# Hybrid decoder step on one core: cached keys scored by page groups of all sequences, with queries as weights and the compression on two row halves

## The reference, cut to what matters

```
k_cmp, v_cmp, k_sel, v_sel = cached pages (4096 rows) + new rows      # 2 key heads x 64
h  = silu(first half of a 32-row block @ w1[:1024] + second half @ w1[1024:] + pe @ w1)
kc, vc = h_k @ w2_k, h_v @ w2_v                      # 255 blocks of 32 rows, stride 16
p_cmp = softmax(q . kc + bias);   o_cmp = p_cmp @ vc
block importance from p_cmp -> top 16 blocks of 64 rows
o_sel = softmax over the chosen blocks of q . k_sel;  o_win = softmax over the last 512 rows of q . k_win
o = gate0*o_cmp + gate1*o_sel + gate2*o_win
```

## Time and profile before

| | us |
|---|---|
| median of 3 runs | 3118.72 (3117.09 to 3127.64) |
| the profiled execution | 3124.01 |
| its span, first to last instruction | 3122.1 |
| `sample_scores`, layer 1, first transpose to last copy | 278.7 to 580.0 |
| the same, layer 2 | 1815.3 to 2115.7 |
| PE busy over the span | 2809.9 (90%) |
| DVE, ACT, POOL busy | 1064.2 (34%), 680.6 (22%), 221.2 (7%) |
| DMA | 274 MB, mean 88 GB/s |

### The profile page before, as it was taken

The page is one execution under the profiler, slowest core; times in us unless marked ns, Lnnn a source line. Parts: engine busy times, 40 slices in busy tenths (PEclk is TensorE's granted clock), DMA queues, the critical chain, the costliest instruction groups (busy, mean ns, idle before and its releaser), DMA issues. The chain is left out here.

```text
span 3122.1 us, 40922 instructions
## 1 busy us (share of the span) xinstructions
PE 2809.9 (90%) x14512; PEld 2232.4 (72%) x14512; DVE 1064.2 (34%) x2653; ACT 680.6 (22%) x1592; POOL 221.2 (7%) x242
## 2 busy tenths in 40 slices
PE   6997999699598999999969889996986989999997
PEld 4875777567585788888758677774665858888886
DVE  2833555445444210000118245554445332100002
ACT  0113444223421110000111244442233103000002
POOL 0500000000040100000005000000001201000000
PEclk8997999889795999999979989997996969999998
DMA  6214556144001225023042065532420011340220
GB/s 192 70 41 156 168 168 188 41 125 122 3 3 27 82 68 162 27 54 81 0 134 81 23 203 189 175 124 67 121 81 2 21 57 58 95 122 25 70 54 29
DMA packets 334997, 274.00 MB, mean 88 GB/s; under 512 B 52866, under 2 KB 330563, under 8 KB 334459
## 3 DMA queue, kind: packets, MB, share of 16 engines
q1 hardware_dynamic: 308296, 251.58, 27.0%
q10 hardware_dynamic: 26546, 20.35, 2.2%
HBM read 262.01 MB, written 18.17 MB: 90 GB/s over the span
## 5 line engine op out<-in xcount | busy, mean ns | idle before, releaser
L2190 PE MATMUL psum<-xT,up_ring 128*128 128x272 f32 x2048 | 470.3, 392 | 0.0
L2190 PEld LDWEIGHTS psum<-xT,up_ring 128*128 128x128 f32 x2048 | 389.4, 190 | 80.0
L2209 PE MATMUL psum<-ff,HT 128*128 128x272 f32 x1536 | 353.6, 393 | 0.0
L2209 PEld LDWEIGHTS psum<-ff,HT 128*128 128x128 f32 x1536 | 292.1, 190 | 59.9
L366 PE MATMUL psum<-xT,w_ring 128*128 128x272 f32 x1408 | 327.0, 395 | 7.0 <-PEq L161 4.0
L366 PEld LDWEIGHTS psum<-xT,w_ring 128*128 128x128 f32 x1408 | 269.6, 192 | 64.2 <-issue 4.7
L1015 PE MATMUL psum<-chunks,W 128*128 128x512 f32 x512 | 242.2, 635 | 10.6 <-DVE chunks L1137 10.6
L1137 DVE COPY chunks<-psum 64x256 f32<-64x256 f32 x512 | 215.2, 420 | 28.9 <-PE psum L994 21.6
L994 PE MATMUL psum<-cst,cache 128*128 128x128 f32 x1536 | 193.5, 278 | 20.8 <-DMA cache<-in_cache_nsa_kv 20.6
L2053 DVE SCALAR_TENSOR_TENSOR xT<-xT,psum 128x544 f32<-128x544 f32 (+1 forms) x42 | 24.2, 585 | 529.7 <-PE psum L2209 441.6
L1015 PEld LDWEIGHTS psum<-chunks,W 128*128 128x128 f32 x512 | 102.5, 203 | 138.6 <-issue 138.6
(11 more groups left out here) (421 smaller groups left out, 3307.2 us busy)
## 6 DMA issues: line engine op xcount, KB each, us to landing
cache<-in_cache_nsa_kv SPq DMA_DIRECT2D x512, 192.0 KB, 3.3
up_ring<-in_w_up SPq DMA_DIRECT2D x32, 1024.0 KB, 5.3
vsel<-in_cache_nsa_kv SPq DMA_DIRECT2D x384, 64.0 KB, 1.9
HT<-in_w_down SPq DMA_DIRECT2D x12, 2048.0 KB, 9.0
w_ring<-in_w_in SPq DMA_DIRECT2D x20, 1024.0 KB, 5.1
vsel<-in_cache_nsa_kv ACTq DMA_DIRECT2D x128, 64.0 KB, 2.3
HT<-in_w_out SPq DMA_DIRECT2D x8, 1024.0 KB, 6.7
yT<-in_w_down SPq DMA_DIRECT2D x4, 2048.0 KB, 10.5
```

Source lines behind the costliest of these rows:

```text
L2190: last = pe.matmul(psum[:, 2 * (t % 4) + h, 0:HALF], up_ring[:, g % 3, k, (t % 2) * P:(t % 2) * P + P], xT[:, k, half_of(h)], start=(k == ...
L2209: last = pe.matmul(psum[:, 2 * (t % 4) + h, 0:HALF], down[t % 3][:, k, :], f[:, k, half_of(h)], start=(k == 0), stop=(k == FT - 1))
```

## The change

Work is regrouped from sequences to page groups. A unit is 4 pages of one sequence; 8 units (one per sequence) cover the same 4 page numbers of all sequences, four units make a quad, 16 quads make the layer, and two more quads hold the window keys. Everything is written out; there is no loop over sequences. In a quad TensorE makes for each unit 12 transposes into banks 0, 1, 2 (one set in place of two), and after each unit's transposes a quarter of the compression of the quad before; after the second unit it also scores the quad before.

- Scores: the queries of a sequence are the weights (32 columns: 16 of them, and zeros in place of the other sequence of the pair), the 512 turned keys are the moving data, and the four units of a quad write four strips of 32 rows of one PSUM bank. Two quads accumulate into the same bank, so it then holds the scores of all 128 query rows, and one copy by VectorE takes them.
- Compression: 64 rows per matmul. Head 0 uses rows 0 to 63 and head 1 rows 64 to 127 of the array, with weights stored twice, and the two heads write two banks. 128 moving columns: 32 blocks of each of the four units.
- `chunks` is filled by one copy of 128 rows in place of four of 64.
- Blocks at a group's edge need the last block of the group before: a small `carry` tile and two small GpSimd adds per quad.
- The prompt's compression and the position term become "quad -1" of the same stage and leave `natural_keys`. Stage "q" goes; GpSimd places the queries in `natural_keys`, and copies out the values that the attention needs later.
- The weights of the first layer are loaded twice (8 DMAs in place of 4).
- "top" gains the second layer of the values (16 matmuls) and loses two transposes; "soft" loses 36 transposes, and adds the block bias in one instruction of 4096 columns.

```diff
 def compression_loads(S, l, sp, s):
-    sp.dma_start(S.pe_n[:, :], layer(io.cmp_pe, l).rearrange("c (h j t) d -> (c h j) (t d)", h=2, j=8)).then_inc(s.cmp, 16)
+    for k in range(KVH):
+        sp.dma_start(S.pe_n[:, HD * k:HD * k + HD], layer(io.cmp_pe, l).rearrange("c p d -> (c p) d")).then_inc(s.cmp, 16)
...
+            for k in range(KVH):
+                sp.dma_start(S.W1[HD * k:HD * k + HD, c, :, HD * h:HD * h + HD], src).then_inc(s.cmp, 16)
...
 def natural_keys(S, l, ctx):
+            for k in range(KVH):
+                r = slice(64 * k, 64 * k + 64)
+                for g in range(GRP):
+                    q = H(T_Q + g)[r, SEQ:].rearrange("p (b t) -> p b t", b=NB)
+                    pool.tensor_copy(rows[r, :, k, g, :], q).then_inc(s.placed, 1)
+                    for o in range(2):
+                        pool.tensor_copy(pads[r, o, o, :, k, g, :], q[:, o::2, :]).then_inc(s.placed, 1)
...
+            pool.tensor_copy(S.kvn[:, :, 0:P], kvn[:, :, 3 * P:4 * P]).then_inc(s.values, 1)
...
 def sample_scores(S, l, ctx):
+    gp, slots = 4, 3
...
+            def turn(u):
+                pe.wait_ge(loaded[u % slots], arrived[u])
+                for bank, c in enumerate((2, 0, 1)):
...
+                    for j in range(gp):
+                        last = pe.transpose(psum[:, bank, j * P:j * P + P], cache[:, u % slots, j, c * P:c * P + P], C["ident"])
+                last.then_inc(s.turned, 1)
+
+            def score(q):
...
+                for i in range(4):
+                    u = 4 * q + i
+                    last = pe.matmul(psum[32 * i:32 * i + 32, 3, :], S.q_pad[:, seq(u), :], kts[u % 8], start=(q % 2 == 0), stop=(q % 2 == 1))
+                last.then_inc(s.scored, 1)
+
+            def compress(q, part):
+                c = part // 2
...
+                n = NP if q < 0 else P
+                for j in range(8 * (part % 2), 8 * (part % 2) + 8):
+                    for k in range(KVH):
+                        r = slice(HD * k, HD * k + HD)
+                        last = pe.matmul(hidden(q, k, c), W1[r, c, j, :], chunks[q % 2][r, c, j, 0:n],
+                                         start=(j == 0), stop=(j == 15))
...
+            for q in range(NQD + 2):
+                for i in range(4):
+                    turn(4 * q + i)
+                    if i == 1 and q:
+                        score(q - 1)
+                    if q <= NQD:
+                        compress(q - 1, i)
+            for i in range(4):
+                keys(i)
+            prompt_second()
+            score(NQD + 1)
+            cmp_score()
...
 def sample_softmax(S, l, ctx):
+            for i in range(4):
+                j = i // 2
+                for n in range(4):
+                    b = 4 * (i % 2) + n
+                    last = pe.matmul(psum[:, 4 + i, n * P:n * P + P], S.hid[:, 1, b, j * P:j * P + P], S.W2[:, 1, :], start=True, stop=True)
...
-            for q in range(NQ):
-                dve.wait_ge(s.turned, q + 1)
-                dve.tensor_tensor(p_sel[:, 512 * q:512 * q + 512].rearrange("p (j n) -> p j n", n=64),
-                                  psum[:, q % 4, :].rearrange("p (j n) -> p j n", n=64), bc(block_bias[:, 8 * q:8 * q + 8], 64),
-                                  ALU.add).then_inc(s.added, 1)
+            x = p_sel[:, 0:PAST].rearrange("p (j n) -> p j n", n=64)
+            dve.tensor_tensor(x, x, bc(block_bias[:, 0:NBLK], 64), ALU.add).then_inc(s.added, 1)
```

More of the change, by code:

```diff
@@ L803, in natural_keys @@
     H = lambda t: S.HT[:, t - 6, :]
[L804 to L813, removed]
+    kvn = sb("kv_rows", [P, QT, 6 * P], ctx=ctx)
@@ L835, in _ @@
                              C["ident"][0:M_W, 0:M_W]).then_inc(s.turned, 1)
[L836 to L849, removed]
         @block.scalar
@@ L856, in _ @@
                 act.wait_ge(s.turned, q + 1)
[L857 to L864, removed]
+                act.copy(dst, psum[0:n, 2 * (q % 4), :]).then_inc(s.copied_act, 1)
             act.wait_ge(s.copied_dve, QT + 1)
@@ L876, in _ @@
                 dve.wait_ge(s.turned, q + 1)
[L877 to L888, removed]
-                                      ALU.add).then_inc(s.added, 1)
-            dve.wait_ge(s.second, 2)
-            dve.tensor_copy(kc[:, :], psum[:, 6, 0:31]).then_inc(s.kept, 1)
-            dve.tensor_copy(vc[:, :], psum[0:31, 7, 0:P]).then_inc(s.kept, 1)
+                dve.tensor_copy(dst, psum[0:n, 2 * (q % 4) + 1, 0:256])
+                dve.tensor_copy(S.misc_n[0:n, q, :], psum[0:n, 2 * (q % 4) + 1, 256:256 + M_W]).then_inc(s.copied_dve, 1)
         @block.sync
@@ L912, in sample_scores @@
     H = lambda t: S.HT[:, t - 6, :]
-    S.q_rows = sb("q_rows", [P, P], ctx=ctx)
-    S.st_cmp = sb("st_cmp", [P, 2, P], ctx=ctx)
-    with stage(nc, "q", "zero", "placed") as (block, s):
+    gp, slots = 4, 3
+    NQD = 2 * (NPG // gp)
+    NU = 4 * (NQD + 2)
+    W1, W2, hid = S.W1, S.W2, S.hid
+    cache = sb("cache", [P, slots, gp, 3 * P], ctx=ctx)
+    second = sb("chunks", [P, 2, 16, P], ctx=ctx)
+    chunks = (S.st_sel[:, :, :].rearrange("p (c j) n -> p c j n", c=2), second)
+    kts = ([S.vc[:, j, 4 * i:4 * i + 4, :].rearrange("p b n -> p (b n)") for j in range(2) for i in range(2)]
+           + [S.yT[:, 4 + i, 0:4 * P] for i in range(4)])
@@ new lines, in sample_scores @@
+    kcs = [cache[:, i, :, :].rearrange("p j n -> p (j n)")[:, 0:512].rearrange("p (b n) -> p b n", b=2) for i in range(2)]
+    kcs += [second[:, i, 0:4, :].rearrange("p j n -> p (j n)").rearrange("p (b n) -> p b n", b=2) for i in range(2)]
+    hb = S.st_win[0:HD, :, :].rearrange("p (k c) n -> p k c n", k=KVH)
+    carry = sb("carry", [HD, 2, 2, KVH, 2, 4], ctx=ctx)
+    hc = sb("hc", [P, 2, 31], ctx=ctx)
+    NP = 34
+    names = ("turned", "k_copied", "v_copied", "sel_act", "sel_dve", "scored", "sc_copied", "tok", "pe_turned", "pe_copied",
+             "comp", "half", "added", "carried", "kept", "zero", "swish", "p_added", "pe_h", "p_swish", "p_second", "p_kept",
+             "kc", "kc_act", "kc_dve", "cmp_scored", "loaded0", "loaded1", "loaded2")
@@ new lines, in add @@
+            def add(q):
+                dve.wait_ge(s.half, q + 2)
+                if q < 0:
+                    for k in range(KVH):
+                        a = pair(q, slice(0, HD))[:, k, :].rearrange("p (c n) -> p c n", c=2)
+                        b = hb[:, k, :, :].rearrange("p c n -> p (c n)")[:, 0:2 * NP].rearrange("p (c n) -> p c n", c=2)
+                        r = slice(HD * k, HD * k + HD)
+                        dve.tensor_tensor(S.pe_h[r, :], a[:, :, 32], b[:, :, 33], ALU.add).then_inc(s.pe_h, 1)
+                        dve.tensor_tensor(hc[r, :, :], a[:, :, 0:31], b[:, :, 1:32], ALU.add).then_inc(s.p_added, 1)
+                    return
+                g, o = q // 2, q % 2
+                for k in range(KVH):
+                    a = pair(q, slice(0, HD))[:, k, :].rearrange("p (c i n) -> p c i n", c=2, i=4)
+                    b = hb[:, k, :, :].rearrange("p c (i n) -> p c i n", i=4)
+                    dve.tensor_tensor(hid[HD * k:HD * k + HD, :, o::2, 32 * g + 1:32 * g + 32], a[:, :, :, 0:31], b[:, :, :, 1:32],
+                                      ALU.add).then_inc(s.added, 1)
+                if g:
+                    dve.wait_ge(s.carried, 2 * q - 2)
+                a = pair(q, slice(0, HD)).rearrange("p k (m n) -> p k m n", n=32)
+                dve.wait_ge(s.zero, 1)
+                dve.tensor_copy(carry[:, (g + 1) % 2, o, :, :, :].rearrange("p k c i -> p k (c i)"), a[:, :, :, 31]).then_inc(s.kept, 1)
@@ new lines, in take_scores @@
+            def take_scores(g):
+                dve.wait_ge(s.scored, 2 * g + 2)
+                dst = S.p_sel[:, 512 * g:512 * g + 512] if g < NPG // gp else S.p_win[:, 0:512]
+                dve.tensor_copy(dst, psum[:, 3, :]).then_inc(s.sc_copied, 1)
+            dve.wait_ge(s.pe_turned, 1)
+            for c in range(2):
+                src = psum[:, 5, 32 * c:32 * c + 32].rearrange("p (h j) -> p j h", h=2)
+                dve.tensor_copy(second[:, c, :, 32:34], src).then_inc(s.pe_copied, 1)
@@ new lines, in _ @@
+            for u in range(NU):
+                q, i = u // 4, u % 4
+                dve.wait_ge(s.turned, u + 1)
+                if u % 2:
+                    if u >= 8:
+                        dve.wait_ge(s.scored, q - 1)
+                    dve.tensor_copy(kts[u % 8], psum[:, 0, :]).then_inc(s.sel_dve, 1)
+                if paged(u):
+                    if q >= 1:
+                        dve.wait_ge(s.comp, 2 * q)
+                    dve.tensor_copy(chunks[q % 2][:, 1, :, 32 * i:32 * i + 32], psum[:, 2, :].rearrange("p (n j) -> p j n", j=16)).then_inc(s.v_copied, 1)
+                if i == 1 and 1 <= q <= NQD + 1:
+                    add(q - 2)
+                if i == 2 and q and q % 2 == 0:
+                    take_scores(q // 2 - 1)
@@ L1237, in sample_softmax @@
     NQ = NPG // 4
```

(2 more changed lines are left out.)

448 lines of the change are left out of this document (185 added, 263 removed).

## The result

The changed kernel takes 3032.6 us (median of 4 runs, 3020.5 to 3042.2) against 3123.2 for the kernel before beside it: ratio 0.970, 95% interval 0.964 to 0.976. It is faster by 3.0%, where the sum of the forecast said 0.3%.

What follows compares the result with a forecast made beforehand. TensorE was taken to bound the scores stage. Each of two layers: stage +2.5 us (304 against 301.3), surroundings -7.7; from 3124.0 profiled this gives 3114, or 3109 on the median's scale. Range of 8 in 10: 3030 to 3380.

Steps and rivals of the forecast that it cites:

- starts keep their order: TensorE's queue: instructions start in program order, so a compression burst fills 17 steps and a quad's four score strips five.
- first window quad and tail: End of the scores stage: 13.0 us for the first window quad, 16.5 for window units, keys and remaining scores.
- half clock elsewhere: Scores stage: stretches at half clock add 5 us a layer, with ends 0 and 12.
- Sharing of the array: Compression: the two row halves work side by side, 7.6 us a quad where in order they would take 14.3.
- no sharing: Main rival, chance 0.22: neighbouring tiles or their weight loads run one after the other, +263 us, 3381.
- Strips: Compressed scores of a quad: eight instructions of 512 columns in five overlapping steps, 2.1 us; in order 3.4.
- Better than counted: Rival, chance 0.13: strips in two steps, cheaper tile changes, no half clock; stage 269 us, program 3039.
- Changes of shape: TensorE switching tile shape nine times a quad: 0.17 us each, 1.5 us a quad (ends 1.1 and 1.7).
- Copies: Copies after each unit's transposes cost nothing behind 2.1 us of compression; uncovered, up to 1.4 us a unit.
- Loads: Page loads with three slots in place of four stay hidden, with 11 us of lead.
- the clock rival: Rival, chance 0.02: half-array work counted as idleness holds the scores stage near half clock, over 100 us a layer.
- Around the stage: Outside the scores stage: first transpose 5.2 us earlier, "soft" 2.5 us less, "top" 0; together -7.7 a layer.

Runs made afterwards that it cites:

- blocks of 2, 4 and 8: Changed kernel with the two heads' compression matmuls alternating in blocks of 2, 4 or 8 in place of 1: 3047.2, 3140.8 and 3240.9 us.
- the run with five banks and two bursts: Changed kernel with transposes rotating over five banks, compression in two bursts a quad, and 128 columns for the prompt's blocks: 2997.9 us.
- one burst a quad: Changed kernel with five rotating transpose banks, 128 columns for the prompt, and a quad's compression in one burst in place of four: 3075.4 us.

## Why the prediction was wrong, step by step

The bound was right: TensorE set the pace before and after. The size was not, and the direction only in part: the sum said 0.3% faster, the chances leaned to slower (0.47 against 0.40), and 3032.6 lies 3 us inside the fast end of the range. The step that failed is that "starts keep their order", for strips "a strip's two instructions follow each other in the queue": a waiting instruction was to hold back the next tile's. By it the four strips of a quad were costed at five steps, 2.1 us, and the compression at 17 steps a burst. They take two steps, 0.9 us, and 16 steps: the runs with blocks of 2, 4 and 8, and the starts of the strips, show an instruction passing up to three that wait for another tile.

| per layer, us | forecast | measured |
|---|---|---|
| 48 transposes of a quad | 5.23 | 5.2 (48 x 0.109) |
| compression of a quad | 4 x 17 steps, 7.6 | 4 x 16 steps, 7.2 |
| strips of a quad | 5 steps, 2.1 | 2 steps, 0.9 |
| changes of shape in a quad | 1.5, and 0.3 for semaphores | 1.5 for both (what is left of 14.77) |
| quad | 16.8 | 14.77 |
| fifteen quads | 252 | 221.5 |
| first quad | 17 | 23.4 |
| first window quad and tail | 13.0 + 16.5 | 22.4 |
| half clock elsewhere | 5 | 0 |
| stage | 304 | 267.4 |

- **Sharing of the array**: right. The main rival, no sharing (3381), is what the compression in blocks of 8 comes near to, with 29 steps of 32; the strips still share there, and the program takes 3240.9.
- **Strips**: 1.2 us a quad too dear, 19 us a layer over the 16 groups ahead of the tail, and again in the tail, where two score groups and the compressed scores were counted at 6.4 and take 3.1. This is the largest part of the 36 us by which the stage was missed. "Better than counted", with a chance of 0.13, had the two steps, and its 3039 is 6 us from the time. That closeness is in part luck: it took 0.4 a quad off the changes of shape, which stayed as counted, and left out the compression's step, the 0.3 for semaphores and the 6.4 that the first quad lost. The rows of before could not show which of the two cases held.
- **Compression**: one step in 17, 0.45 us a quad. The Trainium skill (TensorE: Matmul & The Clock Gate, Part 3: Packing small matmuls) led me to weigh 9.3 us a quad, by a speedup of 3.07 for four tiles; two halves reach 2.0 here. The same section says that matmuls start strictly in program order. For these, two instructions each, the starts do not bear that out: 17 steps with blocks of 2, where order would need 25.
- **Changes of shape**: 0.17 each was right, and the run with five banks and two bursts prices a burst less at 0.34.
- **Copies**: right that they are hidden, and by what. Without the burst between two units PE is idle for 0.77 us, twice a quad.
- **Loads**: right that they are hidden; the margin rests on the bursts between units, as one burst a quad shows.
- **Clock**: 0.96 as before, but in another place. The dips in each sequence are gone, and the first quad lies at half clock for some 21 us with PE never idle. I had put 5 us on the first and 3, with arrivals, on the second; the 5 that were saved and the 6.4 by which the first quad ran over nearly cancel. That the clock rival cost over 100 us is refuted, but it had a real form in the first quad, worth some 16 us of the program.
- **Around the stage**: from the conv stage's last copy to the first transpose 20.2 us against 27.8 (249.84 to 270.08; before 250.96 to 278.74), -7.5 for -5.2: counted from that copy, the stage ahead ends some 0.8 sooner than I had it (the first instruction of the scores stage is at 264.42), the first page issue follows in 0.75 for 1.7 (265.17), and the first transpose in 4.9 for 5.5. From the stage's end to the maximum 13.5 against 17.1 (537.5 to 551.02; before 580.0 to 597.13), -3.6 for -2.5: "top" gave 0.7 that I had not counted (its last instruction ends 7.2 after the stage, before 7.9). Some 1.1 us more lie ahead of the conv stage's last copy; I have no cause for them.

## What to carry to other kernels

When small matmuls sit on different row or column tiles, count the passes of each tile for itself and interleave the tiles one matmul at a time; here the order alone is worth some 200 us. Each switch between tile shapes has a price, so merge what has one shape, but look first at what the piece in between was hiding: copies and loads both came out once it was gone. And read the granted clock of the first stretch of a stage apart from the mean.

## What was not expected of the hardware

- Four column strips of 512 columns cost as much as one: 1.00 us against 0.98.
- Blocks of 34 columns are no faster than blocks of 128 at the same clock: pairs start 0.213 us apart at 1.2 GHz in both, so the 94 columns of zeros cost nothing by themselves.
- The reach of the queue is short: three waiting instructions are the most that any run shows passed, blocks of 4 matmuls need 7 steps more than the 16 of alternation, blocks of 2 one more.
- A PE busy without a gap for 23.37 us, the first quad, was granted a mean clock of 0.54.
